# Hybrid decoder step on one core: Strassen activation sums moved from GpSimd into VectorE's recurrence steps, first branch-B projection with the contraction outermost, reloads queued in another order

## The reference, cut to what matters

```python
xn = rms_norm(x, norm_g)
x_lru, z_lru, q, k, v, z_gla, a_lo, gate_logits = split(xn @ w_in)
xc = causal_conv(x_lru)                                   # width 4
r, i = sigmoid(xc_block @ w_r + b_r), sigmoid(xc_block @ w_i + b_i)
h = scan(h = a * h + u),  a = exp(-8 r softplus(-lam)),  u = sqrt(1 - a*a) * i * xc
y_a = (h * silu(z_lru)) @ w_lru_o                         # branch A
o = gated_linear_attention(q, k, v, decay(a_lo @ w_a2))
y_b = (rms_norm(o) * silu(z_gla)) @ w_gla_o               # branch B
g_a, g_b = split(sigmoid(gate_logits + b_merge))
out = x + (g_a * y_a + g_b * y_b) @ w_out;  y = rms_norm(out)
```

## Time and profile before

| what | value |
|---|---|
| time, median of 3 runs | 1158.12 us (1157.64 to 1159.48) |
| the profiled execution, its time | 1158.47 us |
| its span | 1156.8 us |
| mean granted TensorE clock | 0.983 |
| TensorE busy | 1113.7 us (96%) |
| VectorE busy | 656.4 us (57%) |
| ScalarE busy | 462.9 us (40%) |
| GpSimd busy | 232.7 us (20%) |
| DMA moved | 91.98 MB, mean 80 GB/s |

### The profile page before, as it was taken

The page is one execution under the profiler, slowest core; times in us unless marked ns, Lnnn a source line. Parts: engine busy times, 40 slices in busy tenths (PEclk is TensorE's granted clock), DMA queues, the critical chain, the costliest instruction groups (busy, mean ns, idle before and its releaser), DMA issues.

```text
span 1156.8 us, 17908 instructions
## 1 busy us (share of the span) xinstructions
PE 1113.7 (96%) x7001; PEld 1078.8 (93%) x7001; DVE 656.4 (57%) x838; ACT 462.9 (40%) x643; POOL 232.7 (20%) x140
## 2 busy tenths in 40 slices
PE   8999999995799999999999999999969989999997
PEld 7999999994799999999999999999969989998886
DVE  6677788888744435745855764685444242434433
ACT  6355555444333425446435644633532111112211
POOL 5621122263221121111120211121012120210000
PEclk9999999998899999999999999999989998999999
DMA  6212222211233222102210310221173112342332
GB/s 216 67 57 81 61 60 60 60 50 70 73 115 112 97 95 74 39 19 78 74 36 25 107 38 18 87 63 37 59 281 102 53 38 73 111 137 75 100 109 73
DMA packets 99678, 91.98 MB, mean 80 GB/s; under 512 B 4392, under 2 KB 89256, under 8 KB 99640
## 3 DMA queue, kind: packets, MB, share of 16 engines
q1 hardware_dynamic: 90684, 82.41, 23.1%
q10 hardware_dynamic: 8956, 9.06, 2.4%
HBM read 69.86 MB, written 21.60 MB: 79 GB/s over the span
## 4 chain that ended last, share of the span: by engine, by line
PE 90%; DVE 5%; issue 2%; ACT 1%; DMA 1%; DVEq 0%; ACTq 0%; SPq 0%
PE ps L672 23%; PE ps L673 23%; PE ps L674 23%; PE ps L840 4%; PE ps L841 4%; PE ps L842 4%; PE ps L878 2%; PE ps L920 1%; PE ps L912 1%; PE ps L922 1%; PE ps L905 1%; DVE hh L1716 1%; PE ps L869 1%; DVE act_s L1739 1%; DMA ngb<-in_norm_g 1%
## 5 line engine op out<-in xcount | busy, mean ns | idle before, releaser
L672 PE MATMUL ps<-xn,whi 128*128 128x364 f32 (+1 forms) x1056 | 355.3, 336 | 1.2 <-DVE xn L1605 1.2
L674 PE MATMUL ps<-xn,wlo 128*128 128x364 f32 (+1 forms) x1056 | 346.6, 328 | 0.0
L673 PE MATMUL ps<-xn,whi 128*128 128x364 f32 (+1 forms) x1056 | 346.5, 328 | 0.0
L604 POOL TENSOR_TENSOR wlo<-raw,whi 128x1024 fp32r<-128x1024 f32 x60 | 157.8, 2630 | 672.6 <-ACT whi L1137 672.4
L672 PEld LDWEIGHTS ps<-xn,whi 128*128 128x128 f32 x1056 | 199.1, 189 | 3.5 <-issue 1.5
L673 PEld LDWEIGHTS ps<-xn,whi 128*128 128x128 f32 x1056 | 199.2, 189 | 0.2
L674 PEld LDWEIGHTS ps<-xn,wlo 128*128 128x128 f32 x1056 | 198.7, 188 | 0.0
L1137 ACT ACTIVATE whi<-raw 128x1024 fp32r<-128x1024 f32 x58 | 61.0, 1052 | 114.9 <-PE ps L674 82.2
L672 PE MATMUL ps<-act_s,whi 128*128 128x364 f32 (+1 forms) x192 | 64.1, 334 | 8.9 <-DVE act_s L1739 8.9
L672 PE MATMUL ps<-act_h,whi 128*128 128x364 f32 (+1 forms) x192 | 64.1, 334 | 5.1 <-DVE act_h L2079 5.1
L840 PE MATMUL ps<-tf,whi 128*128 128x272 f32 x192 | 57.4, 299 | 7.7 <-DVE alo L1761 5.3
(11 more groups left out here) (310 smaller groups left out, 2136.0 us busy)
## 6 DMA issues: line engine op xcount, KB each, us to landing
raw<-in_w_in SPq DMA_DIRECT2D x56, 512.0 KB, 4.0
branch_a_in<-keep SPq DMA_DIRECT2D x8, 546.0 KB, 3.5
hzs<-branch_a_in SPq DMA_DIRECT2D x8, 546.0 KB, 8.8
mal<-gate_a SPq DMA_DIRECT2D x8, 544.0 KB, 3.7
xt<-in_x_prompt SPq DMA_DIRECT2D x8, 512.0 KB, 7.6
st<-in_state_gla ACTq DMA_DIRECT2D x4, 1024.0 KB, 5.3
out<-st ACTq DMA_DIRECT2D x4, 1024.0 KB, 4.4
raw<-in_w_gla_o SPq DMA_DIRECT2D x8, 512.0 KB, 3.6
```

Of the source, the lines that this page charges most:

```text
L604: pool.tensor_tensor(wlo[:, c % 2], raw[:, c % 2], whi[:, c % 2].bitcast(F32), ALU.subtract).then_inc(s["lo_ok"], 1)
L672: pe.matmul(dst, wh, mh, start=first, stop=False)
L673: pe.matmul(dst, wh, ml, start=False, stop=False)
L674: return pe.matmul(dst, wl, mh, start=False, stop=last)
```

## The change

- `x_block` goes from GpSimd to VectorE. X11, X22 and X12 are summed behind LRU steps 2, 3 and 4, T1 behind step 4 too, T3 behind step 5, T2 within step 6 ahead of its recurrence. X22 gets a place of its own (`x22`, in the two free tiles at `o_work`). X21 and T4 stay behind step 7, both on VectorE. LRU steps 2 to 5 of VectorE are written out; only steps 0 and 1 stay in the loop. One counter, `hz_out`, counts all stores of `keep`, and each store waits for the one before.
- The split of `aw` goes to the start of the LRU, on ScalarE and on VectorE.
- ScalarE behind the LRU: `gate_a(0)` (it waits for six `t_sum` counts), then T2, T1, `gate_a(1)`, and T3 only behind the tails. VectorE makes the lo of T2 ahead of S1, and that of T1 ahead of the second piece of `alo`.
- The first YB job runs k outermost: for each k tile the three pieces, and it waits for `act_lo` k + 1 alone.
- SyncE: a third `w_gla_o` block is loaded ahead of the reloads, `hzs` comes first, then the fourth block, then `keep` and `mal`. `hz_lo` waits less, and in the YB loop both `hz_lo` stand ahead of the second `branch_b`.

```diff
-            pool.wait_ge(s["hz_out"], 16 * (KT - 2))
-            x_block(T3, 0, 1)
-            x_block(T1, 0, 0)
-            x_block(T2, 1, 1)
-            form_lo(0)
-            pool.wait_ge(s["hz_late"], 32)
-            x_block(T4, 1, 0)
...
+            with dve.Fori(0, 2) as i:
+                lru_step(i)
+            lru_step(2)
+            dve.wait_ge(s["hz_out"], 32 + ONE)
+            x_block(tsum[:, T1], 0, 0)
+            lru_step(3)
+            x_block(x22[:, :, :], 1, 1)
+            lru_step(4)
+            dve.wait_ge(s["hz_out"], 64 + ONE)
+            x_block(tsum[:, T3], 0, 1)
+            t_sum(T1, tsum[:, T3], tsum[:, T1], 3)
+            lru_step(5)
+            t_sum(T3, x22[:, :, :], tsum[:, T3], 4)
...
             input_scale(KT - 2, dec)
+            dve.wait_ge(s["hz_out"], 96 + ONE)
+            t_sum(T2, x22[:, :, :], tsum[:, T1], 5)
             recurrence(KT - 2, sz, ti, dec)
...
+            act.wait_ge(s["t_sum"], T_SUMS)
             gate_a(0, bankA)
-            t_hi(1, T1)
+            act.wait_ge(s["h_tail"], KT)
+            t_hi(T2)
+            t_hi(T1)
             gate_a(1, bankB)
...
-            pe.wait_ge(s["act_lo"], KT)
-            for j in range(2):
-                pe.wait_ge(gb_tanh[j], 1 + ONE)
-            with pe.Fori(0, KT // 2) as i:
+            pe.wait_ge(s["lo_ok"], N_YB + 1)
+            pe.wait_ge(gb_tanh[0], 1 + ONE)
+            for k in range(KT):
+                pe.wait_ge(s["act_lo"], k + 1)
+                for j in range(PIECES):
+                    ins = piece(N_YB, bankA, act_s, j, (k,))
+            ins.then_inc(s["job_done"], 1)
+            pe.wait_ge(gb_tanh[1], 1 + ONE)
+            job(0, N_YB + 1, bankB, act_s)
+            with pe.Fori(1, KT // 2) as i:
...
-            dve.wait_ge(s["back_in"], 16 * (2 * KT - 2))
+            dve.wait_ge(s["back_in"], 16 * (KT - 2))
             with dve.Fori(1, KT // 2) as i:
+                branch_b(i, 0)
                 for j in range(2):
-                    branch_b(i, j)
                     hz_lo(2 * i + j)
+                branch_b(i, 1)
```

More of the change, by code:

```diff
@@ L536, in _ @@
                 load(N_GB + j, j, w_in[:, :, COL_GB + j * P:COL_GB + (j + 1) * P])
-            for j in range(2):
-                load(N_YB + j, j, w_go_v[:, :, j * P:(j + 1) * P])
-            sp.wait_ge(s["hz_out"], 16 * (KT - 2))
-            sp.wait_ge(s["hz_late"], 32)
+            for j in range(3):
+                load(N_YB + j, j % 2, w_go_v[:, :, j * P:(j + 1) * P])
+            sp.wait_ge(s["hz_out"], 16 * KT + ONE)
             sp.wait_ge(s["ga_out"], 32)
@@ L544, in _ @@
             sp.wait_ge(s["job_done"], N_YB)
+            for i in range(KT):
+                sp.dma_start(hzs[:, i, 1, :], hz_dram[i]).then_inc(s["hz_in"], 16)
+            load(N_YB + 3, 1, w_go_v[:, :, 3 * P:4 * P])
             for i in range(2, KT):
@@ L547, in _ @@
                 sp.dma_start(keep[:, i, 0:NTOK], gates["b"][i][:, 0:NTOK]).then_inc(s["back_in"], 16)
-            for i in range(KT):
-                sp.dma_start(hzs[:, i, 1, :], hz_dram[i]).then_inc(s["back_in"], 16)
             for j in range(2):
                 sp.dma_start(mal[:, j, 0:NTOK], gates["a"][j][:, 0:NTOK]).then_inc(mal_in[j], 16)
-            with sp.Fori(1, KT // 2) as i:
+            with sp.Fori(2, KT // 2) as i:
                 for j in range(2):
@@ L652, in form_lo @@
                 pool.tensor_tensor(wlo[form_slot(f)], weights_of(f), whi[form_slot(f)].bitcast(F32), ALU.subtract).then_inc(s["fa_lo"], 1)
[L654 to L661 removed]
+            for f in range(NF * NP):
                 if FORMS[f % NF] in PLAIN:
@@ L1527, in hz_hi @@
                 act.activation(act_h[:, 0, i, :], hzs[:, i, 1, :], ACT.Copy).then_inc(s["act_hi"], 1)
-            with act.Fori(0, KT // 2) as i:
+            for j in range(2):
+                act.wait_ge(s["job_done"], N_YB + 1 + j)
+                hi(0, N_YB + 2 + j)
+            act.wait_ge(s["hz_in"], 16 * KT)
+            hz_hi(0)
+            hz_hi(1)
+            with act.Fori(1, KT // 2) as i:
                 act.wait_ge(s["job_done"], 2 * i + (N_YB + 1))
                 hi(i, N_YB + 2)
-                act.wait_ge(s["back_in"], 16 * (2 * KT - 2))
                 hz_hi(2 * i)
@@ L1721, in recurrence, with x_block, t_sum, lru_step @@
                 dve.tensor_copy(tails[:, i, T_H + 1:T_H + 1 + NSEQ], hh[:, SEQ + SLEN - 1:NTOK:SLEN]).then_inc(s["h_tail"], 1)
[L1723 to L1726, removed]
+            def x_block(dst, k, n):
+                ks, cols = slice(k * KH, (k + 1) * KH), slice(n * HT, (n + 1) * HT)
+                dve.tensor_tensor(dst, xn[:, 0, ks, cols].bitcast(F32), xn[:, 1, ks, cols].bitcast(F32), ALU.add).then_inc(s["t_sum"], 1)
+            def t_sum(form, left, right, after):
+                dve.wait_ge(s["t_sum"], after)
+                dve.tensor_tensor(tsum[:, form], left, right, ALU.subtract).then_inc(s["t_sum"], 1)
+            def lru_step(i):
                 gated_input(i, ti)
```

77 lines of the change are left out of this document (35 added, 42 removed).

## The result

The changed kernel takes 1125.24 us (median of 4 runs, 1124.54 to 1125.50), the kernel before 1158.09 beside it (4 runs, 1157.64 to 1159.48): a ratio of 0.9713, 95% interval 0.9697 to 0.9730. That is 32.9 us less where 33.1 were forecast, and 1125.24 where 1125 was said. The profiled execution took 1125.5 us, its span is 1123.8 us, the mean granted clock 0.995.

The account below looks back on a forecast made before the run. TensorE, busy 96%, bounds the kernel, so time comes only from its gaps and half-clock stretches. Terms 14.6 + 11.1 + 7.4 = 33.1 us off 1158.5 give 1125.4, said as 1125; range 1122 to 1128 (0.68).

Parts of the forecast that it names:

- gain behind the LRU: From the last LRU steps to product 3: 14.6 us less, range 11 to 17.
- gain at the first YB job: First YB job, k outermost, overlaps the making of `act_s` tiles: 11.1 us less, 2.8 of it from half clock.
- gain at the first YA job: Both `hz_lo` ahead of the last `branch_b` remove a 5.1 us wait and 2.3 of clock loss: 7.4 us less.
- moves into the LRU steps: Sums behind LRU steps 2 to 5 cost nothing if they fit VectorE's 5.16 us idle ahead of each gated input.
- step (2): T2 within LRU step 6: VectorE's multiply meets GpSimd's weight split, so the scan starts near 246.9, 1.3 us lost.
- step (6): S1 to U2 on VectorE takes 17.0 us instead of 19.7; U2 at 287.6, 15.6 us gained.
- Step (1): Last LRU steps on VectorE: without GpSimd's blocks the scan, product and copy give back 13.7 us.
- more than forecast: Rival, chance 0.08: VectorE's multiply precedes the weight split and the clock doesn't fall behind product 3; 1120 to 1122 us.
- Steps (3) to (5): Behind the LRU: last `tails` copy at 261.2, `gate_a(1)` ends at 266.4, S1 at 270.6, gain 13.0 us.
- The clock behind product 3: Product 3 begins near a clock fall, now costing 1.7 us; possibly more after a longer wait, 1.0 us taken off.
- 24 changes of PSUM bank cost clock: Rival, chance 0.05: small holes at bank changes put the whole first YB job at 1.2 GHz; 1137 us.
- The queue: SyncE's reloads, 10.3 MB in 26 us from 844.3: weight blocks land in time for YB; no term in the sum.

Follow-up runs that it names:

- the second of these kernels: Changed kernel with the last block sum and T4 ahead of S1, and `alo` ahead of T3's high and T1's low part: 1117.29 us.

## Why the prediction was right

| step of the prediction | forecast | measured |
|---|---|---|
| scan of step 6 starts | 246.9 | 246.23 |
| last `tails` copy | 261.2 | 260.4 |
| `gate_a(1)` ends | 266.4 | 265.5 |
| S1 | 270.6 | 269.6 |
| from S1 to U2 | 17.0 | 17.8 |
| U2 | 287.6 | 287.5 |
| gain behind the LRU | 14.6 | 14.6 |
| gain at the first YB job | 11.1 | 10.9 |
| gain at the first YA job | 7.4 | 7.5 |
| moves into the LRU steps | 0 | 0 |

The total is near by some luck: step (2) was too dear by about as much as step (6) was too cheap.

**Step (1), the lock**, held: the same scan takes 2.43 us wherever GpSimd's sums aren't beside it, in the changed kernel and in the one with the sums held back. The Trainium skill has the mechanism, on its page "SBUF — State Buffer" under "SBUF: two separate sides": VectorE and GpSimd share a pair of ports as an exclusive lock, and whichever begins first has it for its whole instruction; for a VectorE op outside the two-port modes this holds when it has two inputs in SBUF and GpSimd's op reads SBUF. The rows agree, 7.05 against 2.43 us for one scan, which has two inputs there.

**Step (2), T2 within step 6,** was 0.6 us too dear. VectorE's multiply was to stand for GpSimd's weight split. It doesn't, and didn't in the kernel before: the op of eight columns behind it stands. The multiply and that op before, then the multiply in the changed kernel:

```profile
241.91 1.30 DVE L1709 TENSOR_TENSOR ti<-ti,wt 128x1092 f32<-128x1092 f32 x1 [1.48 <-ACT wt L1221]
243.24 2.26 DVE L1713 TENSOR_TENSOR ti<-ti,fix 128x8 f32<-128x8 f32 x1
...
242.59 1.28 DVE L1713 TENSOR_TENSOR ti<-ti,wt 128x1092 f32<-128x1092 f32 x1
```

In both traces the split ends 2.26 us behind the multiply's end (245.47 and 246.13, ends of the multiply 243.21 and 243.87). In the changed kernel the split shows 3.33 us in place of 2.57, for it is GpSimd that stands longer, behind the multiply. So the scan is late by what the multiply is late, 0.7 us, not 1.3; most of T2's 2.42 us went into the 1.48 us that VectorE had idled there. That was half of the rival "more than forecast"; its other half, no fall of the clock, did not come.

**Steps (3) to (5)** carried this on: 0.8 us early at the last `tails` copy and at `gate_a(1)`, 1.0 at S1.

**Step (6), from S1 to U2,** was 0.8 us too cheap, and hid the first error. VectorE waited 1.0 us for ScalarE's `alo`, behind ScalarE's 1.5 us of issuing the four stores of `trow`, ScalarE's rows in the changed kernel:

```profile
269.54 1.52 ACTq L1301 DMA_DIRECT2D out<-trow  x4
271.11 0.94 ACT L1284 ACTIVATE alo<-ps 32x364 fp32r<-32x364 f32 x2 [1.60 <-issue]
```

S1's own standing and the lo of T2 had covered that before; the forecast took both away and left the wait out. The 0.6 us added for a weight split was not needed: the `x_block` did meet one and took 2.92 us, but before it was the sum of T4 that met it, 2.92 us at 299.52, and this was in the 19.7 already. T4 now takes 2.42. The price of an `x_block` on VectorE, open between 2.36 and 5.9, is 2.41 to 2.43 us where GpSimd is quiet. **The clock behind product 3**: 1.0 us was taken off for a longer fall. U2 gained 15.8 and the `act_s` tiles 14.6, so 1.2 went. TensorE's wait for U2 is the 3 to 5 us forecast (5.0), the one for `alo` shorter than the 2 to 3 forecast (1.7).

**The moves into the steps** cost nothing, and the experiment with three more sums shows that this was a matter of room, not of kind.

**First YB job.** The wait shrank from 8.9 to 0.5 us, and 2.5 of the 10.9 came from the clock (2.8 in the prediction, though the 12 us at 0.78 of the earlier trace rows give 2.6). The rival that 24 changes of PSUM bank cost clock fell: the clock is 1.00 in each window of the job. What the prediction set against the loop order from the Trainium skill ("TensorE: Matmul & The Clock Gate", "A second HAM failure mode: psum-queue depth-cycling") did not come: 72 matmuls in three banks in turn ran in 11.9 us, the same as a job in order. That is no case against the page, which tells of a kernel whose TensorE idles often between groups. In this job the matmuls behind the first start 0.16 to 0.17 us apart, with no such gap, so it shows only that changing banks without a gap costs nothing here.

**The queue** was put at nothing in the sum, rightly for the whole change. The prediction named the place, the third block that came just in time before, but gave no price for leaving it there: it is 10.4 us, nearly all of the gain at YB.

**First YA job.** The wait of 5.1 us and the fall behind it are gone, by the order of `hz_lo`, as the kernel with that order undone shows.

What stays open: why two of the kernels with one part undone (the whole YB job, the order of `hz_lo`) stand 1.8 us ahead of the changed kernel's trace by 820 us, though nothing in their programs ahead of that differs (the `act_s` tiles end at 836.0 in both and at 837.8). Most of it lies behind product 3, where the same wait of 4.99 us was followed by half clock up to 294.3 in the changed kernel and up to 290.9 in the one with the order of `hz_lo` undone; what decides that wasn't found.

## What to carry to other kernels

An instruction that is long in one place and short in another, on the same shape, is standing for something: look at what the neighbour engine runs in just that time, and move that work, not only its start, since holding it back moved a wait of 10 us from the transposes of `tails` to product 0 and gained nothing. Follow a standing engine to the end of the stretch: here the split that met an added sum had met the convolution before, and the net cost was 2.1 us less than the sum's row showed. When a transfer's order and a loop's order are changed together, try each alone: here either alone is worth nothing and the pair is worth 10 us. Size a move ahead by the idle time left between it and what sets the end, not by how far its first instruction moves.

## What the runs showed of the hardware

- An op of VectorE over eight columns, 0.17 us by itself, took 2.26 us beside a weight split of GpSimd, and a copy of eight columns 4.80 beside a block sum: the size of the op that stands does not matter here, what is left of the other one does. It goes both ways: the same split showed 2.57 us when it began 0.3 us before the end of VectorE's multiply and 3.33 when it began 1.1 before.
- The same code had waits of TensorE at product 1 of 1.71, 1.74 and 1.75 us with the clock at 1.00 behind them, and of 1.82 and 1.93 us with about 3.4 us at 0.50. The length alone does not order them: at product 3 a wait of 2.11 us (the kernel with the LRU part undone) left the clock at 1.00, one of 2.37 (the kernel before) did not. In the five runs of the kernel with T4 early, three have a clock of 0.999 and spans of 1116.3 to 1116.8, two 0.997 and spans of 1117.5 and 1117.7. The trace is of one of the latter, with the fall behind product 1, so it is likely, not shown, that this 1 us hangs on whether the clock falls there. In the second of these kernels, without that wait, the five runs agree to 0.5 us.
- Four DMA issues on ScalarE's queue took 1.52 us of its time, and the `alo` work behind them began 1.60 us after the last op ahead of them, with nothing else to wait for.
